# Constants ahead of the weights, norms among the first sums, and single row steps placed more finely in a two-block kernel

## The reference, cut to what matters

```python
cond = silu(c)
for i in range(4):                        # kinds: GLA, SGU, FoX, GLA
    shift, scale, gate = split(cond @ w_mod[i] + b_mod[i], 3)
    h = rms_norm(x, norm_pre_g[i]) * (1 + scale) + shift
    x = x + gate * rms_norm(mixer_i(h), norm_post_g[i])
# gla_mixer: a_low = h @ w_in[..., 16 last columns]; decays from a_low @ w_a2 + b_a
# second block
h = x + hybrid_mixer(rms_norm_2(x, norm_mix), ...)
# peer_ffn(u): per token 8 heads choose 16 of 16384 experts each
a = gelu(sum_d(u * expert_down[idx]))     # 128 picks per token
y = sum_picks(gates * a * expert_up[idx])
out = rms_norm_2(h + y, final_norm)
```

## Time and profile before

| | us |
|---|---|
| median of 3 runs | 1698.29 (1695.9 to 1699.72) |
| the profiled execution's own time | 1696.64 |
| its span in the trace | 1694.9 |
| PE busy | 1350.4 (80%) |
| DVE busy | 1038.9 (61%) |
| POOL busy | 483.5 (29%) |
| ACT busy | 433.6 (26%) |
| HBM read | 590.08 MB, 349 GB/s over the span |

### The profile page before, as it was taken

One profiled execution on the slowest core, in us unless ns is written; L12 is line 12 of the kernel. 1 busy time (PEld: TensorE's weight loads), 2 busy tenths in 40 slices (PEclk: granted clock), 3 DMA queues, 4 the chain that ended last, 5 costly groups with the idle time before them and its releaser, 6 DMA issues. The chain is left out here.

```text
span 1694.9 us, 13321 instructions
## 1 busy us (share of the span) xinstructions
PE 1350.4 (80%) x3934; PEld 675.0 (40%) x3934; DVE 1038.9 (61%) x2172; ACT 433.6 (26%) x976; POOL 483.5 (29%) x482
## 2 busy tenths in 40 slices
PE   2799978899998999998978669699588646766665
PEld 1354445454444554444543334455234312222222
DVE  5456544644232213116788986898855877778776
ACT  2122323426324321011333232222011221111111
POOL 1101111110000000003445645455444543454441
PEclk9899989999999999999978889798799878888988
DMA  9979896976757677879989989999999999999996
GB/s 380 395 285 380 334 358 223 377 300 245 249 189 270 249 260 260 309 260 353 412 313 416 414 316 413 402 415 414 413 416 414 342 413 420 421 420 421 420 420 260
DMA packets 108828, 592.02 MB, mean 349 GB/s; under 512 B 12211, under 2 KB 12467, under 8 KB 60501
## 3 DMA queue, kind: packets, MB, share of 16 engines
q0 software_dynamic: 67520, 312.52, 46.2%
q1 hardware_dynamic: 41236, 278.65, 43.0%
HBM read 590.08 MB, written 1.05 MB: 349 GB/s over the span
## 5 line engine op out<-in xcount | busy, mean ns | idle before, releaser
L967 PE MATMUL bank<-ring,hT 128*128 128x512 f32 x1888 | 864.0, 614 | 37.9 <-DVE hT L1848 12.9
L967 PEld LDWEIGHTS bank<-ring,hT 128*128 128x128 f32 x1888 | 365.2, 197 | 479.2 <-issue 458.6
L896 POOL DMA_INDIRECT room<-in_peer_down,idx x92 | 101.6, 1104 | 540.8 <-DVE idx L1772 411.9
L1790 DVE CUSTOM_DVE_ANT_0 room<-room 128x1024 f32<-128x1024 f32 x180 | 218.8, 1221 | 58.3 <-DMA room<-in_pair,idx 41.6
L1195 PE MATMUL bank<-room 128*128 128x512 f32 x284 | 159.6, 710 | 97.8 <-ACT room L1486 95.8
L1805 DVE SCALAR_TENSOR_TENSOR x<-room,pcoef,x 128x1024 f32<-128x1024 f32 x121 | 155.7, 1286 | 27.2 <-DMA room<-in_peer_up,idx 26.5
L896 POOL DMA_INDIRECT room<-in_peer_up,idx x104 | 116.7, 1122 | 87.8 <-DVE pa L1790 40.0
L1195 PEld LDWEIGHTS bank<-room 128*128 128x128 f32 x284 | 61.0, 227 | 195.7 <-issue 101.1
L896 POOL DMA_INDIRECT room<-in_pair,idx x88 | 99.5, 1131 | 114.2 <-PE bank L1195 61.2
L946 PE MATMUL bank<-cst,room 128*128 128x128 f32 x424 | 64.7, 296 | 79.0 <-DVE room L1529 40.5
L870 POOL DMA_DIRECT2D room<-in_wmod x80 | 42.2, 528 | 257.8 <-DVE modr L1552 170.2
(11 more groups left out here) (295 smaller groups left out, 1425.8 us busy)
## 6 DMA issues: line engine op xcount, KB each, us to landing
ring<-in_wpk SPq DMA_DIRECT2D x248, 1024.0 KB, 7.5
room<-in_wmod POOLq DMA_DIRECT2D x80, 512.0 KB, 8.8
room<-in_wmod SPq DMA_DIRECT2D x8, 1024.0 KB, 17.2
room<-in_norm_post_g POOLq DMA_DIRECT2D x4, 512.0 KB, 5.1
rowb<-in_gate_bias SPq DMA_DIRECT2D x4, 512.0 KB, 8.9
room<-in_peer_up,idx POOLq DMA_INDIRECT x104, 13.0
room<-in_peer_down,idx POOLq DMA_INDIRECT x92, 13.8
room<-in_pair,idx POOLq DMA_INDIRECT x88, 14.2
```

What stands on the lines that cost most here:

```text
L896: return pool.indirect_dma_start(out=dst, out_offset=None, in_=A[table][0] if table != "pair" else A[table], in_offset=bass.IndirectOffset ...
L967: last = mm(bank[p][:, :], lhs, ring[:, h % 4, k * N:(k + 1) * N], start=(kk == 0), stop=(h == halves[-1] and k == 3))
L1790: v.tensor_tensor_reduce(out=row, in0=row, in1=u_(g // MINE), scale=1.0, scalar=0.0, op0=ALU.mult, op1=ALU.add, accum_out=pa[:, g // TOPK ...
```

## The change

1. `wlow` and `wa2` are issued directly behind the eight early pairs, ahead of the first four weight halves; `wlow` has a semaphore of its own, `low_in`, and `low` on PE waits for that. The four others of `consts_in` stay ahead of `("mm", 0, "in0", 2)` (value 64), and the two `rowb` rows go ahead of `("mm", 0, "out0", 0)`.
2. `x` of tile 0 and tile 1 is loaded behind the first and the second pair of pieces (before: the second and the third). DVE sums six pieces, does the norm of tile 0, sums two more, then does the norm of tile 1 (before: eight pieces, both norms).
3. `spot(1)` is called also between two levels and between `quad_V` and the next `quad_S`.
4. Of the last eight picks PE adds 248, 250, 251, 252, 253, and DVE 249, 254, 255 (before, 251 was DVE's). 248 to 251 are added at tick 271 (before 272 and 273), 252 and 253 at 273 (before 274), and the last group of two becomes two of one, so that 254 is added a tick earlier.
5. Two semaphores become one, `dve_set`.

```diff
 def on_vector(u):
-    return u < 7 * TOPK or (u % 4 == 3 and u < PICKS - 4) or (u % 2 and u < MINE) \
-        or u >= PICKS - 2 or (u % 2 and PICKS - 8 <= u < PICKS - 4)
+    return u < 7 * TOPK or (u % 4 == 3 and u < PICKS - 8) or (u % 2 and u < MINE) or u >= PICKS - 2 or u == PICKS - 7
 def added_at(v):
+    if v >= PICKS - 2:
+        return tick_of(v) + 2
     if v >= PICKS - 8:
-        return tick_of(PICKS - 2) + (v - PICKS + 8) // 2
+        return tick_of(PICKS - 2) - 1 + 2 * ((v - PICKS + 8) // 4)
     return tick_of(v) + LEAD[v // MINE]
-    + [(PICKS - 4, 2), (PICKS - 2, 2)]
+    + [(PICKS - 4, 2), (PICKS - 2, 1), (PICKS - 1, 1)]
...
             if (s[0], after[0]) in (("quad_S", "quad_P"), ("cross", "heads")):
                 spot(2)
+            elif (s[0], after[0]) in (("level", "level"), ("quad_V", "quad_S")):
+                spot(1)
...
                 load(early[i], A["wmod"][2 * i:2 * i + 2].rearrange("a p n -> p a n"), early_in(i))
-                if 1 <= i <= T:
-                    load(x[:, i - 1, :], A["x"][0, (i - 1) * P:i * P, :], f"x_in{i - 1}")
+                if i < T:
+                    load(x[:, i, :], A["x"][0, i * P:(i + 1) * P, :], f"x_in{i}")
+            load(wlow[:, :, :, :], A["wlow"], "low_in")
+            load(wa2[:, :], A["wa2"][:, 0, :], "wa2_in")
...
                     if step == ("mm", 0, "in0", 2):
-                        load(wlow[:, :, :, :], A["wlow"], "consts_in")
-                        load(wa2[:, :], A["wa2"][:, 0, :], "wa2_in")
                         load(cst[:, CST_FIRST:CST_N], A["cst"][:, CST_FIRST:CST_N], "consts_in")
                         load(gmask[:, :, :], A["gla_mask"], "consts_in")
                         load(wsT, A["wsT"], "consts_in")
                         load(posi[:, :], A["pos"], "consts_in")
+                    if step == ("mm", 0, "out0", 0):
                         load(rowb[:, 0, :], A["sgu_ln_g"].to_broadcast([P, D]), "rowb_in")
                         load(rowb[:, 1, :], A["sgu_ln_b"].to_broadcast([P, D]), "rowb_in")
...
                 elif kind == "low":
-                    pe.wait_ge(S("consts_in"), 80)
+                    pe.wait_ge(S("low_in"), 16)
...
                 elif kind == "first":
-                    for n in range(KC if t == 0 else 0):
+                    for n in ((0, 1, 2, 3, 4, 5), (6, 7))[t]:
                         add_piece(n)
                     normalize(t, 0)
```

More of the change, by code:

```diff
@@ L1080, in _ @@
                     pe.wait_ge(S(f"ln{t}"), 2)
-                    pe.wait_ge(S("wsT"), 1)
+                    pe.wait_ge(S("dve_set"), 1)
                     for g in range(SG):
@@ L1087, in _ @@
                 elif kind == "forget_sum":
-                    pe.wait_ge(S("consts_in"), 80)
+                    pe.wait_ge(S("consts_in"), 64)
                     for j in range(t + 1):
@@ L1423, in _ @@
                         if n < 4:
-                            act.wait_ge(S("gqk"), 1)
+                            act.wait_ge(S("dve_set"), 2)
                         af(k_T(t, n)[rows, :, :].rearrange("p h n -> p (h n)"), bank[c][rows, :], ACT.Copy,
@@ L1668, in angles @@
             def angles():
-                dve.wait_ge(S("consts_in"), 80)
+                dve.wait_ge(S("consts_in"), 64)
                 link(v.tensor_copy(posf[:, :], posi[:, :]))
@@ L1819, in _ @@
                     L = t
-                    for n in range(KC if L == 0 else 0):
-                        add_piece(KC + n)
+                    for n in range(KC, 2 * KC if L == 0 else KC):
+                        add_piece(n)
                     mod_columns(L)
@@ L1919, in _ @@
                     if t == 0:
-                        dve.wait_ge(S("consts_in"), 80)
-                        dve.wait_ge(S("consts_in"), 80)
+                        dve.wait_ge(S("consts_in"), 64)
+                        dve.wait_ge(S("consts_in"), 64)
                         v.tensor_tensor(wsT, wsT, summ.unsqueeze(1).to_broadcast([P, SG, P]), ALU.mult) \
-                            .then_inc(S("wsT"), 1)
+                            .then_inc(S("dve_set"), 1)
                     dve.wait_ge(S("rowb_in"), 32)
@@ L1967, in _ @@
                     if t == 0:
-                        v.tensor_tensor(gqk[:, :], const("gq"), const("gk"), ALU.mult).then_inc(S("gqk"), 1)
+                        v.tensor_tensor(gqk[:, :], const("gq"), const("gk"), ALU.mult).then_inc(S("dve_set"), 1)
                 elif kind == "quad_T" and t == 0:
@@ L1973, in _ @@
                     if n < 4:
-                        dve.wait_ge(S("gqk"), 1)
+                        dve.wait_ge(S("dve_set"), 2)
                         ins = v.tensor_scalar(dst[0:FW, :], bank[c][0:FW, :], gqk[0:FW, :], None, ALU.mult)
```

## The result

The changed kernel takes 1710.89 us (median of 4 runs, 1709.68 to 1711.94) against 1697.61 for the kernel before, timed beside it (4 runs): ratio 1.0085, 95% interval 1.0059 to 1.0110, some 14 us slower. The profiled execution took 1711.94 us, its span 1710.2.

A forecast was written before the change was run, and what follows sets the result against it. DMA was taken to bound the kernel to about 100 us, PE to about slice 18, then DMA again. Start -7.9, ticks -1 and end +1.7 summed to -7.2 us: 1691 us, range 1680 to 1700.

The forecast's parts named there:

- Ticks placed more finely: Tile 0's ticks spread from out2 to hyb 14: filling idle DMA against lengthening DVE's chain, taken as -1 us.
- The slower rival: At eight new spots a tick delays the DVE step others wait for: +18.7 us, 1711 in all; chance 0.11.
- The second hole: DMA idle time in 980 to 1000 us, 8.4 us, blamed on DVE's tickless levels and POOL's 6.83 us wait.
- The start: First projection to in0 3: low waits for wlow alone, in0 3 ends at 75.4 instead of 83.3, -7.9 us.
- in0 1 and in0 2 run in the slack: Before in0 3: these two chunks fit ahead of its second weight half, forecast to land at 71.9 us.
- The last rival: Start gains nothing: in0 2's first half comes late or the clock falls again; about 1700, chance 0.05.
- I expect no further wait: Behind in0 3: PE has more work for each MB, so no more waits for weights; no size given.
- The rival's sum for the start: Start gives back only bytes, as POOL's pieces delay in0 3's last half: start 4.1 us, 1695 in all; chance 0.14.
- Carried to the end: A shift of the PE-bound stage moves the ticks' start and the DMA-bound rest by the same amount.
- x, norms, rowb later: Before the first projection and ahead of out0 0: reordered loads and norms, later rowb rows, all costed at 0.
- The end: Tail behind the last gather: PE also adds pick 251, DVE waits for PE before the final addition, +1.7 us.

The follow-up runs named there:

- the execution of start and end: The changed kernel without the two finer-spot lines, so only its start and end edits, against the kernel before: ratio 1.0001.
- the last two starts: Kernel before with the change's start edits and weight pieces moved: four sums from ahead of in0 3's levels, 0.9964; then two more pieces, 0.9956.

## Why the prediction was wrong

- **Ticks placed more finely: the step that failed.** It took -1 of bounds -20.2 to +18.7; the runs say +16 for this part alone. I took from DVE's 18.35 of 20 us that nothing was left to fill, and put the time that five ticks add to the levels (11.7 us) equal to what they take off later. Both sides of that balance were wrong. The levels grew by 18.3 us, 13.5 of waits and 4.9 of PE's busy time; with the three ticks at the quads, which I had not priced apart, PE's lag rose by 32.9 us from 774.8 to 1033.9, more than the bound for all eight ticks. Taken off were 22 us by 1108, and 11 us were lost again behind that. What remained, 14 us at 1326, is the loss. (By the earlier trace rows a tick is 2.43 us, 981.74 less 979.31, and not 2.34; that changes little.)
- **The slower rival** (1711) named direction and place; it had 0.11. Its number came out by luck: it adds a start of -7.9 that measured -3, a tail of +1.7 and 18.7 for ticks, whose price isn't 2.34 us each and isn't a sum. What I held against it, "DMA is full in most of that stretch, so ticks pay there", didn't follow: DMA was still full in 960 to 980 us (412 GB/s), ran dry 40 us behind (283 and 278 GB/s), and had done so at 880 to 920 us too (296 and 333 GB/s).
- **The second hole** (980 to 1000 us) was put down to levels without ticks and to POOL's wait. With ticks in the levels the wait is still there, 6.14 us, and the hole larger. In the kernel before DVE waits at the heads' step only 0.79 us, with other work ahead of it. That the hole hangs on the ticks around that step is my reading; the run with two of them moved ahead speaks for it, with the limits said there.
- **The start: a number right by luck.** Forecast were low at 47 us in 1.9 us and in0 3 ending at about 75.4; measured low at 45.5 us in 1.92 us, and in0 3 ending at 76.0. But the lead of 7.3 against 7.9 came about another way. "in0 1 and in0 2 run in the slack" was wrong: in0 2 waited 2.73 us for its first half and ran in 9.98 us, at the lower clock at first, and in0 3's second half, which I had made the bound at 71.9, was there at 69.5. The last rival named that place and the clock, for a loss of the whole lead; it took 5.6 of 12.9 us. "I expect no further wait" behind in0 3 holds for weights and fails for DVE's pieces, which I had set against the weights only, as a rival, and not against DVE's own queue. With the pieces out of the way the lead was 8.2. By the rule of the Trainium skill (DMA: Bandwidth & Descriptors, section Issuing engines are not separate DMA queues) the pieces share the DMA engines with the halves. The trace agrees: the three pieces shown landed 1.40 to 2.44 us after DVE was free for them, with DMA at 399 to 438 GB/s. The rival's sum for the start (-4.1) is near the measured -3, but not by its mechanism: it had nothing at in0 2, where 5.6 us of lead went, nor at DVE's pieces behind in0 3, where 3.6 more went.
- **Carried to the end.** Not 1:1. In the changed kernel's trace the lead is 3.7 us behind the levels, 6.1 at the 600th instruction and 0.5 at 775 us, in single chunks that ran at another granted clock than in the kernel before (one of 8.83 us at 548 us instead of 7.13, with 0.88 and 0.78 granted in 545 to 555 us instead of 1.00). Executions whose start is that of the kernel before stand at the same 600th instruction between -5.4 and +2.5 us, so a lead of this size can't be followed through single traces. Of the 8.2 and 9.9 us of the last two starts 6 and 7.5 arrive by the ratios.
- **x, norms, rowb later:** taken at 0. In the changed kernel's trace PE's first projection starts at 36.73 us and runs in 8.82 us, before at 36.95 in 10.16, so low came 1.6 us earlier than forecast. In the other traces with this start it took 8.65 to 10.12 us. No run takes these edits apart.
- **The end:** +1.7 forecast. From the last dot product that waits for a gather to the final addition it is 10.57 us before and 10.75 after; DVE waits 1.48 us for PE; a wait was forecast, of about 3 us. PE's sixteen matmuls in 7.03 us are four more than before, but the first four ran in 1.99 us instead of 3.44. In the execution of start and end PE was slower, DVE waited 3.18 us and the same stretch took 12.44. So 0.2 to 1.9; the term was right in kind; its size went with how fast PE ran there.

## What to carry to other kernels

Work put in front of a step that another engine waits for costs at once, even where a transfer is the bound, and it can cost more than its own time: eight ticks of 2.4 us put PE 33 us behind here. What it takes off later can be as large (22 us), so price both sides from the waits of the engine that waits, and not from a busy share. Don't add the prices of parts: either half of the finer spots cost as much as both. When a wait is removed near the start, list what each engine has in front of the next shared step, weights and sums alike, since work that had time to land behind the old wait becomes the new one; and test a schedule in both directions, because here 4 ticks fewer cost nearly as much as up to 8 ticks more.

## What the runs showed of the hardware

PE's clock added to the lag. After waits of 14.66 and 6.32 us the eight small matmuls of a level took 2.08 us, at a granted clock of 0.50 in 962.1 to 964.2 and 985.5 to 987.6 us; at 978 and 996 us, at 1.00, eight took 1.16. The kernel before has this too, but less of it: 3.78 us for sixteen after the 13.08 us, and the granted clock of 980 to 1020 us was 0.83 and 0.81, where the changed kernel had 0.59 in 1000 to 1020. In sum PE was busy 4.9 us longer in the levels. At the start a wait of 2.73 us went with a clock of 0.50 and a chunk of 9.98 us instead of 7.13, one of 1.88 us with a clock of 0.50 in 60 to 62 us and 8.80, and one of 1.44 us with a clock of 1.00 and 7.42. I had counted DVE's ticks at 2.34 us each, and not this.
